# Sample attention: the old rows of the second attention's keys and values land in every fourth partition in place of 32 partitions side by side

## The reference, cut to what matters

```
DIL_PATTERNS = ((128, 1), (512, 4), (2048, 16))      # window, dilation

def dilated_sample(q, kc, vc, buf_len, slopes):
    for window, dil in DIL_PATTERNS:
        steps = jnp.arange(window // dil + 1)
        idx = buf_len + jnp.arange(t_)[:, None] - dil * steps[None, :]
        kg = kc[:, idx_c]; vg = vc[:, idx_c]
        s = einsum(q, kg) * B_HD ** -0.5 - slopes * dil * steps
        ...                                              # softmax, output, log-sum-exp
    return combine_branches(outs, lses)
```

## Time and profile before

| | us |
|---|---|
| median of 3 runs | 3516.17 |
| the profiled execution, its own time | 3519.17 |
| its span, first to last instruction | 3517.6 |
| `attend_sample` in it, about 1337 to 1649 | 312 |

### The profile page before, as it was taken

The page is one execution under the profiler, slowest core; times in us unless marked ns, Lnnn a source line. Parts: engine busy times, 40 slices in busy tenths (PEclk is TensorE's granted clock), DMA queues, the critical chain, the costliest instruction groups (busy, mean ns, idle before and its releaser), DMA issues. The chain is left out here.

```text
span 3517.6 us, 58272 instructions
## 1 busy us (share of the span) xinstructions
PE 3238.6 (92%) x19347; PEld 3006.2 (85%) x19347; DVE 1896.3 (54%) x4302; ACT 1374.1 (39%) x2979; POOL 516.3 (15%) x397
## 2 busy tenths in 40 slices
PE   6999999799989997875996999999999999999997
PEld 5999999688989995443784999999999999999997
DVE  5222222477768883333894564565376447626754
ACT  5111111388867773322543333333333333333332
POOL 0010110154520002332452000100010000001000
PEclk6999999899999998987998999999999999999999
DMA  3333335546357679997676675476467547644442
GB/s 127 122 97 102 120 104 154 149 85 138 79 128 177 162 194 277 316 323 216 209 244 189 186 234 163 138 237 215 125 200 232 174 130 233 203 146 144 118 118 79
DMA packets 638791, 597.21 MB, mean 170 GB/s; under 512 B 38601, under 2 KB 561314, under 8 KB 633442
## 3 DMA queue, kind: packets, MB, share of 16 engines
q1 hardware_dynamic: 608742, 461.72, 46.4%
q10 hardware_dynamic: 10750, 69.92, 5.8%
q0 software_dynamic: 19104, 63.06, 5.5%
HBM read 492.29 MB, written 169.55 MB: 188 GB/s over the span
## 5 line engine op out<-in xcount | busy, mean ns | idle before, releaser
L2426 DVE TENSOR_TENSOR ff_wl<-ff_wr,ff_wh 128x1024 fp32r<-128x1024 f32 (+2 forms) x380 | 404.0, 1079 | 287.2 <-ACT ff_wh L2358 286.7
L2358 ACT ACTIVATE ff_wh<-ff_wr 128x1024 fp32r<-128x1024 f32 (+2 forms) x380 | 349.2, 938 | 249.5 <-PE ff_d L2286 125.1
L450 PE MATMUL pj_acc<-hT_h,pj_wh 128*128 128x416 f32 x960 | 339.9, 354 | 10.0 <-POOL pj_wl L367 10.0
L450 PE MATMUL pj_acc<-hT_l,pj_wh 128*128 128x416 f32 x960 | 337.8, 352 | 0.0
L2284 PE MATMUL ff_g<-ff_hh,ff_wh 128*128 128x416 f32 x880 | 310.4, 353 | 28.8 <-DMA ff_hh<-scratch_h2T 25.5
L2284 PE MATMUL ff_u<-ff_hh,ff_wh 128*128 128x416 f32 x880 | 310.9, 353 | 16.1 <-DVE ff_wl L2426 16.1
L2284 PE MATMUL ff_d<-ff_ah,ff_wh 128*128 128x416 f32 x880 | 313.8, 357 | 10.3 <-DVE ff_wl L2426 10.3
L2286 PE MATMUL ff_g<-ff_hh,ff_wl 128*128 128x416 f32 x880 | 311.1, 353 | 0.9 <-issue 0.9
L2286 PE MATMUL ff_d<-ff_ah,ff_wl 128*128 128x416 f32 x880 | 311.3, 354 | 0.0
L2286 PE MATMUL ff_u<-ff_hh,ff_wl 128*128 128x416 f32 x880 | 310.4, 353 | 0.0
L2285 PE MATMUL ff_g<-ff_hh,ff_wh 128*128 128x416 f32 x880 | 308.8, 351 | 0.0
(11 more groups left out here) (269 smaller groups left out, 7032.6 us busy)
## 6 DMA issues: line engine op xcount, KB each, us to landing
ff_wr<-in_w_gate SPq DMA_DIRECT2D x110, 512.0 KB, 4.2
ff_wr<-in_w_up SPq DMA_DIRECT2D x110, 512.0 KB, 5.0
bx_kca<-in_cache_a_k SPq DMA_DIRECT2D x128, 256.0 KB, 14.1
sa_vca<-in_cache_a_v POOLq DMA_DIRECT2D x128, 256.0 KB, 7.5
out<-in_cache_win_k ACTq DMA_DIRECT2D x64, 511.0 KB, 4.6
out<-in_cache_win_v ACTq DMA_DIRECT2D x64, 511.0 KB, 4.7
ff_wr<-in_w_down SPq DMA_DIRECT2D x80, 384.0 KB, 4.0
ff_wr<-in_w_down SPq DMA_DIRECT2D x80, 320.0 KB, 3.5
```

The lines of the kernel that those rows point to most:

```text
L450: m = pe.matmul(acc[g][:, 0:PG], weights[:, k, c], part[:, c, cols], start=start, stop=stop)
L2358: act.activation(wh[:, slot, 0:size], wr[:, slot, 0:size], ACT.Copy).then_inc(w_hi, 1)
L2426: dve.tensor_tensor(wl[:, slot, 0:size], wr[:, slot, 0:size], wh[:, slot, 0:size].bitcast(F32), ALU.subtract).then_inc(w_lo, 1)
```

## The change

The four transfers of old rows write partitions r, r + 4, r + 8, ... 124 + r in place of 32 r to 32 r + 31. Row 16 * (32 n + g) + r now goes to partition 4 g + r, tile n. The table that says which position a partition holds follows. Everything else, the DRAM side of the transfers too, is as it was: each engine's instructions are the same ones, with the same waits, in the same order (5057 rows on PE, 3128 on DVE, 1365 on ACT, 720 on POOL, 1183 on SP in both). The transfers at line 919 are 64 in number: 8 sequences, keys and values, four remainders.

```
     win = t["cache_" + kind]["b"][seq]
     old = win[0:PAST - 512].rearrange("(n g r) e -> r g n e", n=W_OLD, r=16)
     for r in range(4):
-        eng.dma_start(dst[32 * r:32 * r + 32, 0:W_OLD], old[r]).then_inc(sem_, 16)
+        eng.dma_start(dst[r:P:4, 0:W_OLD], old[r]).then_inc(sem_, 16)
     eng.dma_start(dst[:, W_OLD:], win[PAST - 512:].rearrange("(n p) e -> p n e", p=P)).then_inc(sem_, 16)
...
-    old = 16 * (32 * np.arange(W_OLD)[None] + (p % 32)[:, None]) + (p // 32)[:, None]
+    old = 16 * (32 * np.arange(W_OLD)[None] + (p // 4)[:, None]) + (p % 4)[:, None]
```

## The result

The changed kernel takes 3484.86 us, the median of four runs (3478.41 to 3485.79), against 3515.68 us before (3507.65 to 3527.24). The ratio is 0.9905, 95% interval 0.9882 to 0.9928: 30.8 us faster. The prediction had 3503, with a range down to 3486.

The account below looks back on a forecast made before the run. It took slow old-row transfers to bound the sample stage: 3519.2 - 11.8 (rate) - 1 (ACT's statistics) = 3506.4 for the profiled execution, 3.0 above the median, so 3503; range 3486 to 3520.

Parts of the forecast that it names:

- What bounds the stage: Sample stage: DMA engines never idle but slow at old rows; five sequences lose 31 us, TensorE's transfer waits being 24.7.
- Why the old rows are slow: Old-row loads: a narrow band of partitions uses half the way into SBUF, 200 to 221 GB/s; gapped reading not needed.
- Between the ends I take half: Old rows' rate in the sample stage: half of 34.5 us recovered, 17.2, between nothing and all gained.
- the two short periods: Two sample-stage stretches already lasting 33 us can use no gain: 5.4 us off the 17.2, leaving 11.8.
- The conversion of rate into time: Five sequences: 193 us would take 158.5 at 387 GB/s, 34.5 less; TensorE's 32.3 us a sequence allow 31.
- ACT's issue of the statistics: Two statistics transfers, 16.48 us to issue, stand behind old rows: a gain between 0 and 2 us, taken at 1.
- The first rival: Old rows in the sample stage run at the pages' rate: gain 24 to 31 us plus up to 2, 3489; chance 0.27.
- Its own argument against itself: Sample-stage queues must hold 373 GB/s, close to their best 387, and pages wait for single buffers, so some waits stay.
- Issue cost: SP and GpSimd issuing old rows with a step of four: 0 to 2.2 us more on a sequence's four, taken at 0.
- the old rows of sequence 0's keys: End of attention B: 3.5 us would become 2, under work that does not wait for them, so 0 gain.
- the end of the full spread: Fastest outcomes of old rows running at the pages' rate in the sample stage, left below the range's 3486.
- The likeliest case: Sample stage: part of the time lost at old rows is recovered, 7 to 22 us, 3494 to 3509; chance 0.40.

Follow-up runs that it names:

- the prompt's heads: On top of the changed kernel, six loads of keys and queries in both prompt attentions write every second partition: 3481.62 us, ratio 0.9908; repeated, 3480.99 us, 0.9908.

## Why the prediction was wrong, step by step

- What bounds the stage: right. Engines never idle but slow, at old rows, and three long periods with waits behind them. All of it went when the rate rose.
- Why the old rows are slow: right, and now shown. Not the reading (204 GB/s without gaps), not the neighbourhood (206 GB/s in steps of 2 within a half), but how much of the 128 a transfer reaches (379 GB/s in steps of 4 over all). What in the chip makes it so, the ways in and who shares them, no run shows.
- The step that failed is "Between the ends I take half". It took two engines on one way in to stay a pair in the new layout, meeting half of the time. That was a picture of how a transfer is dealt out to the engines, with no row behind it. The changed kernel runs as if engines never met, 379 GB/s; kernels whose smaller transfers were meant to force such meetings have 245 and 288. Whether its engines have ways of their own or only fall out of step at once stays open. With 34.5 us hanging on the slow stretches the choice of half, less 5.4 for the two short periods, made 11.8 us; measured on the same five periods it is 30.8, which is the whole of the 31 that TensorE's own pace allows.
- The conversion of rate into time held: the ceiling of 32.3 us a sequence was hit to 0.1 us (161.9 for five), and the kernel without most old rows has the same stage, so this is the floor.
- ACT's issue of the statistics: taken at 1 us, between 0 and 2; TensorE's wait fell by 4.84 us (9.05 to 4.21). I had only counted the 4 us of one slow stretch, but ACT's 16.48 us had more in them than that stretch; 5.37 us of them went, nearly all of it with the values' rows alone (11.25 us), where I had looked at SP's.
- The first rival, 3489, was the right mechanism. Its own argument against itself, that 373 GB/s are too close to 387 for all waits to go, was wrong: the periods ran at 361 to 378 GB/s without one wait for a transfer. With that reservation dropped it would have said 31 + 4.8 us off the stage, measured 36.0. The median of runs moved by 30.8. I don't know where the other 5 us lie; the kernel before stood between 3513.8 and 3517.5 in the four comparisons, and single runs of it scatter over some 25 us.
- Issue cost: taken at 0, right for the time. SP needs 602 ns for a transfer in steps of 4 where it needed 429, GpSimd 563 in place of 552, and nothing waits for it. For the rate it was not always 0: I had let the old rows of sequence 0's keys, alone at the end of attention B, pass in 2 us, and they had 270 GB/s and took some 3.8 us, with 0.66 us from one issue to the next. No time hung on it.
- The range: 3486 to 3520 cut off "the end of the full spread", and the result lies 1.1 us outside it. The likeliest case carried 0.40 on a mechanism that no row supported, against 0.27 for the one that the nearest row by span gave.

The row that I should have followed was there: the recent rows of the same window, to all 128 partitions, at 364 GB/s right behind the old ones at 221. Where the cause of a low rate is the span and the change removes just that, the value for the full span is the likeliest one, and half of it needs its own evidence.

## What to carry to other kernels

When the DMA engines' share is over 1 and the rate is half of what other stretches reach, look at which partitions the transfer writes: 32 or 64 partitions within one half of SBUF pass at 200 to 220 GB/s, the same number spread over all 128 at 380 to 416, for an edit that changes a slice and a table. Choose the stride so that one transfer reaches the whole range by itself, and keep 32 partitions or more in it: split into 16, the same layout had 245 and 288 GB/s; two transfers that together do so gain far less (223 to 229 GB/s by turns). Then ask what waits: here the sample stage gave 36 us for it and the prompt's heads nothing that can be measured.

## What the runs showed of the hardware that I had not expected

- A transfer need not fill the partitions to have the full rate: 32 of 128 in steps of 4 with rows of 2 KB reach 379 GB/s, and 64 in steps of 2 with rows of 8 KB reach 416, more than the pages' 387 to 128 partitions.
- The same partitions, cut into transfers of 16, pass at 245 and 288 GB/s, but cut by tile into transfers of 32 partitions and 64 KB they keep the full rate (383 and 386 beside pages). What matters is which partitions, or how many, are in one transfer, and not its bytes, down to 64 KB, as long as the queue holds work ahead.
- Issuing a transfer with a partition step costs SP 602 ns at the median in place of 429:

```profile
L919 POOL DMA_DIRECT2D sa_vcb<-in_cache_win_v x32: 547/563/577, 1365.2 to 1597.6; - x32
L919 SPq DMA_DIRECT2D bx_kcb<-in_cache_win_k x16: 598/602/1382, 1300.1 to 1533.9; - x16
```

- Slow packets of one queue hold up the issue on another: ACT, with transfers of its own that have nothing to do with the window, spent 16.48 us issuing them while old rows were slow, 11.11 us when these were fast, and 11.25 us when only GpSimd's were.
